# Embedding gates by Strassen's algorithm on 2x2x2 blocks: weight block differences on GpSimd, row block sums on VectorE

## The reference, cut to what matters

```python
h = h + jax.nn.sigmoid(h @ ple_w_gate[i]) * (p[i] @ ple_w_proj[i])
```

## Time and profile before

| what | us |
| --- | --- |
| median of 3 runs | 2815.74 (2813.85 to 2818.06) |
| the profiled execution | 2807.85 |
| its span | 2806.0 |
| TensorE matmuls busy | 2567.0 (91%) |
| VectorE busy | 875.4 (31%) |
| ScalarE busy | 568.4 (20%) |
| GpSimd busy | 480.3 (17%) |
| stage_ple, first and second time, about | 351 to 436 and 858 to 943 |

### The profile page before, as it was taken

The page is one execution under the profiler, slowest core; times in us unless marked ns, Lnnn a source line. Parts: engine busy times, 40 slices in busy tenths (PEclk is TensorE's granted clock), DMA queues, the critical chain, the costliest instruction groups (busy, mean ns, idle before and its releaser), DMA issues. The chain is left out here.

```text
span 2806.0 us, 37484 instructions
## 1 busy us (share of the span) xinstructions
PE 2567.0 (91%) x15258; PEld 1356.2 (48%) x15258; DVE 875.4 (31%) x1809; ACT 568.4 (20%) x1341; POOL 480.3 (17%) x682
## 2 busy tenths in 40 slices
PE   7997898988989999889999999959999899989985
PEld 4654444435554454555555555434455454444442
DVE  2306512353251221664111211120556542111112
ACT  2106112232221111631000010021345111000000
POOL 2623210071231121340000000020344200000001
PEclk9998999997999999999999999979999899999997
DMA  5211013110021420125999999951001089999997
GB/s 177 85 66 46 30 35 120 42 41 2 4 77 37 144 90 32 38 77 209 358 411 411 411 411 411 369 193 53 32 32 61 1 337 411 411 411 411 411 411 282
DMA packets 180273, 532.33 MB, mean 190 GB/s; under 512 B 21360, under 2 KB 31472, under 8 KB 180144
## 3 DMA queue, kind: packets, MB, share of 16 engines
q1 hardware_dynamic: 167536, 505.22, 46.5%
q10 hardware_dynamic: 10240, 16.79, 1.6%
q0 software_dynamic: 2368, 8.52, 0.9%
HBM read 507.26 MB, written 23.10 MB: 189 GB/s over the span
## 5 line engine op out<-in xcount | busy, mean ns | idle before, releaser
L344 PE MATMUL psum<-weight_ring,hidden_T 128*128 128x512 f32 (+2 forms) x1216 | 475.9, 548 | 2.7 <-PEq L576 1.6
L344 PEld LDWEIGHTS psum<-weight_ring,hidden_T 128*128 128x128 f32 x1216 | 228.7, 191 | 223.0 <-issue 158.2
L2982 PE MATMUL psum<-arena,hidden_T 128*64 128x512 f32 x1344 | 296.2, 592 | 0.0
L2971 PEld LDWEIGHTS psum<-hidden_T,arena 128*128 128x128 f32 x2304 | 266.8, 192 | 49.6 <-issue 49.6
L2971 PE MATMUL psum<-hidden_T,arena 128*128 128x128 f32 x2304 | 283.3, 278 | 0.0
L2994 PE MATMUL psum<-weight_ring,hidden_T 128*64 128x512 f32 x1024 | 235.4, 602 | 34.1 <-DMA weight_ring<-in_moe_w_down 30.0
L3248 POOL DMA_INDIRECT arena<-expert_rows_out,arena x18 | 20.4, 1133 | 1061.9 <-issue 534.3
L2982 PEld LDWEIGHTS psum<-arena,hidden_T 128*64 128x64 f32 x1344 | 100.5, 137 | 186.9 <-issue 186.9
L2982 PE MATMUL psum<-weight_ring,hidden_T 128*64 128x512 f32 x704 | 155.0, 592 | 0.0
L2994 PEld LDWEIGHTS psum<-weight_ring,hidden_T 128*64 128x64 f32 x1024 | 71.0, 137 | 153.0 <-issue 128.5
L2976 DVE TENSOR_TENSOR hidden_T<-psum,norm_gains 128x512 f32<-128x512 f32 x64 | 44.3, 691 | 293.9 <-PE psum L2982 182.7
(11 more groups left out here) (546 smaller groups left out, 3195.5 us busy)
## 6 DMA issues: line engine op xcount, KB each, us to landing
arena<-in_moe_w_up SPq DMA_DIRECT2D x84, 2048.0 KB, 24.1
weight_ring<-in_moe_w_down SPq DMA_DIRECT2D x64, 2048.0 KB, 24.0
weight_ring<-in_moe_w_up SPq DMA_DIRECT2D x44, 2048.0 KB, 23.4
weight_ring<-in_hg_w_in SPq DMA_DIRECT2D x8, 2048.0 KB, 10.6
weight_ring<-in_ev_w_in SPq DMA_DIRECT2D x8, 1536.0 KB, 6.9
weight_ring<-in_fox_w_in SPq DMA_DIRECT2D x6, 2048.0 KB, 8.1
weight_ring<-in_od_w_in SPq DMA_DIRECT2D x5, 2048.0 KB, 8.0
weight_ring<-in_ple_w_gate SPq DMA_DIRECT2D x4, 2048.0 KB, 9.3
```

The lines of the kernel that those rows point to most:

```text
L344: last = nc.tensor.matmul(out, l, r, start=i == 0, stop=i == len(left) - 1)
L2971: last = nc.tensor.matmul(g.psum[:, c // 4, (c % 4) * P:(c % 4 + 1) * P], keep[:, i, c * P:(c + 1) * P], row[:, i, :], start=i == 0, stop= ...
L2982: last = nc.tensor.matmul(g.psum[64 * q:64 * q + 64, 2 + n, :].rearrange("p (s c) -> p s c", s=2), xT[:, k // 4, k % 4, ROWS * n:ROWS * n ...
```

## The change

Two column halves of one chunk each, two k halves, and the two tiles of a pair make 2x2x2 blocks; seven products of four k blocks each take the place of eight. The weight differences T[0] to T[3] (128x2048) are made by GpSimd from the ring, behind the root of tile 0 and ahead of its additions to g.h; the row sums S (128x512, four for each pair) by VectorE, two of them between the copies of tiles 2 and 3 to g.hT, the other six behind those of tile 4. Product 1 is copied out of PSUM by ScalarE (first) before product 2 adds to the same bank; the other blocks take it from that copy: VectorE adds it to products 6 and 5 as they come (7 and 4 add in PSUM to bank 2 behind 6, product 3 to bank 3 behind 5), and adds what then stands there for 7, 3 and 4 (take). The sigmoid of six of the eight blocks reads and writes SBUF. Turning uses two banks, 6 and 7, one for each half tile, and its semaphores count halves. The order of TensorE is the list steps. Projections keep their number and size; where each stands changes.

```diff
+    copied, taken, summed, weighted = g.sig("values_copied", "bank_read_by_vector", "block_sums_ready", "weight_sums_ready")
     pT = g.take(2, SEQ)
-    gate, gate2 = g.take(2, 512), g.take(2, 512)
+    T = [g.take(4, 512) for _ in range(4)]
+    S = [[g.take(4, P) for _ in range(4)] for _ in range(2)]
+    first, gates = g.take(2, 512), g.take(8, 512)
...
+    pairs = [(1, 2), (3, 4)]
+    operands = [block_products(row_blocks(g.hT, pair), weight_blocks(g, chunks), S[p], T) for p, pair in enumerate(pairs)]
+    bank = lambda n: g.psum[:, n, :]
+    where = lambda n, p: bank(p) if n < 3 else bank(2) if n in (4, 6, 7) else bank(3)
+    steps = [("turn", "raw", 1), ("turn", "raw", 2), (1, 0), ("turn", "raw", 3), (2, 0), ("turn", "raw", 4), ("proj", 0), (1, 1), (2, 1)]
+    steps += [("turn", "norm", t) for t in few] + [("proj", 1), (6, 0), (5, 0), (7, 0), ("proj", 2), (3, 0), ("proj", 3), (4, 0), ("proj", 4)]
+    steps += [(6, 1), (5, 1), ("turn", "norm", 1), (7, 1), ("proj", 5), ("turn", "norm", 2), (3, 1), ("proj", 6), (4, 1), ("proj", 7), ("turn", "norm", 3), ("turn", "norm", 4)]
...
+    blocks = [(0, 2, 0, 0), (1, 2, 0, 0), (0, 7, 1, 1), (0, 3, 0, 1), (0, 4, 1, 0), (1, 7, 1, 1), (1, 3, 0, 1), (1, 4, 1, 0)]
+    block_at = {block[:2]: e for e, block in enumerate(blocks)}
+    value = lambda p, n: gates[:, block_at[p, n], :]
+    takes = [(n, p) for p in range(2) for n in (6, 5, 7, 3, 4)]
+    taken_at = {job: i + 1 for i, job in enumerate(takes)}
+    sums = [(0, 0), (0, 1), (0, 2), (0, 3), (1, 0), (1, 1), (1, 2), (1, 3)]
...
+                for half in range(2):
+                    j = 2 * turn_at[kind, t] + half
+                    if j >= 2:
+                        pe.wait_ge(*moved.at(j - 1))
+                    for c in range(4 * half, 4 * half + 4):
+                        src = rows[0:n, nth[t] % 2, c * P:(c + 1) * P] if kind == "norm" else g.h[0:n, t, c * P:(c + 1) * P]
+                        last = nc.tensor.transpose(g.psum[:, 6 + half, (c % 4) * P:(c % 4) * P + n], src, g.c("identity")[0:n, 0:n])
+                    last.then_inc(*transposed.up())
+
+            def product(n, p):
+                if n == 1:
+                    pe.wait_ge(*moved.at(2 * turn_at["raw", pairs[p][0]] + 1))
+                if n == 2:
+                    pe.wait_ge(*moved.at(2 * turn_at["raw", pairs[p][0]] + 2))
+                    pe.wait_ge(*copied.at(p + 1))
+                if n == 6:
+                    pe.wait_ge(*weighted.at(2))
+                    pe.wait_ge(*summed.at(4 * p + 2))
+                    if p:
+                        pe.wait_ge(*taken.at(taken_at[4, 0]))
+                if n == 5:
+                    pe.wait_ge(*summed.at(4 * p + 1))
+                    if p:
+                        pe.wait_ge(*taken.at(taken_at[3, 0]))
+                if n == 7:
+                    pe.wait_ge(*weighted.at(3))
+                    pe.wait_ge(*summed.at(4 * p + 3))
+                    pe.wait_ge(*taken.at(taken_at[6, p]))
+                if n == 3:
+                    pe.wait_ge(*summed.at(4 * p + 4))
+                    pe.wait_ge(*taken.at(taken_at[5, p]))
+                if n == 4:
+                    pe.wait_ge(*weighted.at(4))
+                    pe.wait_ge(*taken.at(taken_at[7, p]))
+                a, b = operands[p][n]
+                for k in range(4):
+                    last = nc.tensor.matmul(where(n, p), a[:, k, :], b[:, k, :], start=k == 0 and n in (1, 5, 6), stop=k == 3, skip_group_check=n in (2, 3, 4, 7))
+                last.then_inc(*ready.up())
...
+            def copy(p):
+                act.wait_ge(*ready.at(at[1, p]))
+                nc.scalar.activation(first[:, p, :], bank(p), ACT.Copy).then_inc(*copied.up())
+
+            def sigmoid(e):
+                p, n, i, half = blocks[e]
+                if n == 2:
+                    act.wait_ge(*ready.at(at[2, p]))
+                    nc.scalar.activation(gates[:, e, :], bank(p), ACT.Sigmoid).then_inc(*gated.up())
+                else:
+                    act.wait_ge(*taken.at(taken_at[n, p]))
+                    nc.scalar.activation(gates[:, e, :], gates[:, e, :], ACT.Sigmoid).then_inc(*gated.up())
...
+            copy(0)
+            sigmoid(0)
+            for t in few:
                 scale(t)
-            for t in XT:
-                sigmoid(2 * t - 2)
-                if t > 1:
-                    square(t - 1)
-                sigmoid(2 * t - 1)
-                if t > 1:
-                    scale(t - 1)
+            copy(1)
...
+            def row_sum(p, i):
+                (a11, a12), (a21, a22) = row_blocks(g.hT, pairs[p])
+                s = S[p]
+                if i == 0:
+                    dve.wait_ge(*moved.at(2 * turn_at["raw", pairs[p][1]] + 2))
+                else:
+                    dve.wait_ge(*summed.last())
+                x, y, op = ((a21, a22, ALU.add), (s[0], a11, ALU.subtract), (a11, a21, ALU.subtract), (a12, s[1], ALU.subtract))[i]
+                nc.vector.tensor_tensor(s[i], x, y, op).then_inc(*summed.up())
+
+            def take(n, p):
+                dve.wait_ge(*ready.at(at[n, p]))
+                dve.wait_ge(*copied.at(p + 1))
+                dst = value(p, {6: 3, 5: 7}.get(n, n))
+                if n in (7, 3):
+                    dve.wait_ge(*taken.at(taken_at[{7: 5, 3: 6}[n], p]))
+                nc.vector.tensor_tensor(dst, dst if n in (7, 3) else first[:, p, :], where(n, p), ALU.add).then_inc(*taken.up())
...
+            move("raw", 1)
+            move("raw", 2)
+            row_sum(0, 0)
+            row_sum(0, 1)
+            move("raw", 3)
+            move("raw", 4)
+            for job in sums[2:]:
+                row_sum(*job)
+            multiply(0)
+            for t in few:
+                move("norm", t)
+            multiply(1)
+            for p in range(2):
+                for n in (6, 5, 7, 3, 4):
+                    take(n, p)
+                    if n in (7, 3, 4):
+                        multiply(block_at[p, n])
+                    if p and n == 5:
+                        move("norm", 1)
+                    if p and n == 7:
+                        move("norm", 2)
+            move("norm", 3)
+            move("norm", 4)
 
...
+            def weight_sum(dst, x, y):
+                nc.gpsimd.tensor_tensor(dst, x, y, ALU.subtract).then_inc(*weighted.up())
+
+            (b11, b12), (b21, b22) = weight_blocks(g, chunks)
             for t in few:
                 root(t)
-            for t in XT:
-                add(2 * t - 2)
-                if t > 1:
-                    root(t - 1)
-                add(2 * t - 1)
+            g.weights_wait(pool, chunks[0])
+            g.weights_wait(pool, chunks[1])
+            weight_sum(T[0], b12, b11)
+            pool.wait_ge(*weighted.at(1))
+            weight_sum(T[1], b22, T[0])
+            weight_sum(T[2], b22, b12)
+            pool.wait_ge(*weighted.at(2))
+            weight_sum(T[3], b21, T[1])
+            for e in range(5):
+                add(e)
...
```

More of the change, by code:

```diff
@@ L583, in turn @@
                     pe.wait_ge(*scaled.at(nth[t] + 1))
[L584 to L591, removed]
@@ new lines, in project @@
+            def project(e):
+                p, _, i, half = blocks[e]
+                a = TILES[pairs[p][i]][0] - META
+                if e >= 2:
+                    pe.wait_ge(*multiplied.at(e - 1))
+                w = g.weights(proj_chunk)
+                products(nc, bank(4 + e % 2), [pT[:, k, a:a + P] for k in range(2)], [w[:, k, 512 * half:512 * half + 512] for k in range(2)]).then_inc(*proj_ready.up())
+            for s in steps:
+                if s[0] == "turn":
+                    turn(*s[1:])
+                elif s[0] == "proj":
+                    if s[1] == 0:
@@ L604, in _ @@
                         g.weights_wait(pe, proj_chunk)
                         pe.wait_ge(*p_in.at(16))
[L606 to L616, removed]
+                    project(s[1])
+                else:
+                    if s == (1, 0):
+                        g.weights_wait(pe, chunks[0])
+                    product(*s)
+                    if s == (4, 0):
+                        g.chunk_used(chunks[0], ready)
+                    if s == (3, 1):
+                        g.chunk_used(chunks[1], ready)
@@ L647, in _ @@
                 square(t)
+            copy(0)
+            sigmoid(0)
+            for t in few:
                 scale(t)
-            for t in XT:
-                sigmoid(2 * t - 2)
-                if t > 1:
-                    square(t - 1)
-                sigmoid(2 * t - 1)
-                if t > 1:
-                    scale(t - 1)
+            copy(1)
+            for e in (1, 2, 3, 4):
+                sigmoid(e)
+            square(1)
+            square(2)
+            scale(1)
+            scale(2)
+            sigmoid(5)
+            sigmoid(6)
+            square(3)
+            sigmoid(7)
+            scale(3)
             square(4)
```

(6 more changed lines are left out.)

73 lines of the change are left out of this document (23 added, 50 removed).

## The result

| | before | changed |
| --- | --- | --- |
| median, us | 2816.45 (2813.85 to 2818.06, 4 runs) | 2799.81 (2798.76 to 2800.86, 4 runs) |
| ratio | | 0.9942, 95% interval 0.9925 to 0.9959 |
| the profiled execution, us | 2807.85 | 2800.86 |
| its span | 2806.0 | 2799.1 |
| first gate stage, first turning to the next stage's first product | 351.64 to 435.81: 84.17 | 352.68 to 430.83: 78.15 |

The changed kernel is faster, by 16.6 us in these medians, where 9.6 had been forecast. The two profiled executions differ by 7.0 us only, the two gate stages by 6.02 + 4.01 = 10.03.

A forecast was written before the change was run, and what follows sets the result against it. The gate stage was taken as a TensorE chain; 5.80 and 3.83 us saved in two stages, together 9.6, took the profiled 2807.85 to 2798.2, plus 7.9 carried over gave 2806.1 us; range 2802.0 to 2811.0.

The forecast's parts named there:

- Removed work: Gate products on TensorE: 8 fewer matmuls of 0.429 us per pair of tiles, 6.86 us less per stage, 13.7 for two.
- The weight difference: One GpSimd subtraction of 128x2048 in the gate stages: 4.28 us, bounds 3.66 and 5.06.
- The walk: TensorE's queue stepped through each gate stage to the last product's end: 67.43 us in the first, 70.19 in the second.
- Exclusion: GpSimd and VectorE, both inputs in SBUF, take turns by whole instructions; 1.07 us excludes at 512 elements; PSUM copies aren't held.
- no-exclusion rival: Row sums beside differences aren't held up; only 0.86 us lost per stage, gain 13.0, time 2802.7 us; chance 0.20.
- long-differences rival: GpSimd's weight differences take 5.06 us each; gain 4.7 us, time 2811.0; chance 0.08.
- the slower one: Exclusion by elements stretches each difference beside VectorE to 8.3 us; time 2831 us; chance 0.05.
- The two waits before tile 4: TensorE idle before turning tile 4, whose turning needs tile 3's copies behind row sums: 0.65 us first stage, 2.75 second.
- The wait for product 1's copy: TensorE waits before product 2 of pair two for ScalarE's copy of product 1: 0.86 us.
- The tail: From a gate stage's last product to the next stage's first product: the same chain, 10.94 us unchanged.
- part (3): Among what is added in the gate stages: turning a tile handed over by halves, through two banks in place of four.
- The rival's price: Clock rival: second stage's pause before tile 4 costs TensorE its clock, 1.8 us; gain 7.8, time 2807.9; chance 0.25.

The follow-up runs named there:

- the pieces: Each of GpSimd's four 128x2048 weight differences made as four 128x512 instructions, against the changed kernel; 2795.33 us, ratio 0.9939 to the kernel before.
- the kernel that copies first: VectorE copies tiles 3 and 4 before any row sum, against the changed kernel; 2797.71 us, ratio 0.9949 to the kernel before.
- the third: Third profiled execution of the changed kernel, from its third timing with no edit: 2799.99 us, ratio 0.9959 to the kernel before; second stage 82.57 us.

## Why the prediction was wrong

In the stages the mechanism was right. The result fell 2.2 us below the range, mostly by the last step of the sum, which goes from the gain to the median, and for the rest because the gain came out larger.

**Which step failed.** "The median of the runs shown is 2815.74, 7.9 above that execution; the difference is carried over: 2806.1 us." It did not carry over. The changed kernel's median, 2799.81, lies 1.05 us below its profiled execution (2800.86) and not 7.9 above it. This step is 8.9 us too high; the profiled execution itself came out 2.7 us above its forecast of 2798.2, and 6.3 us remain between 2806.1 and 2799.8.

Both ends of the 7.9 were off. The profiled execution of the kernel before was a short one outside the two stages, 2637.0 us against 2642.9 in its second. And the level of 2815.74 came from three runs: 55 later runs of the same kernel, in three groups, have medians of 2810.4 to 2812.5. With 2812.3 the same sum gives 2802.7, inside the range. Counted so, 3.4 of the 6.3 us are level and 2.9 are gain: the stages of the changed kernel save 10.03 where I had 9.6, and the measured gain stands above the stages' by what the section before leaves open. Counted against the kernel before timed beside it (2816.45), all of the miss is gain, 16.6 for 9.6; the later groups, which give 13.8 together, speak for the first count. Why the first group's level is some 4 us above the others isn't shown.

**Removed work**: right. 112 matmul records in place of 128 in each stage, those on sums at 0.43 us as well (24 in 10.46).

**The weight difference**: 4.28 us taken; it is recorded at 4.52 (bounds 3.66 and 5.06), and at 4.84 to 4.96 where a row sum is still running as it starts. The walk came out right nevertheless, because what it used was the part that holds VectorE: row sum 2 took 4.89, 4.21 more than its own 0.68, and 4.28 is four times the 1.07 of the earlier trace rows. The record is 0.3 us longer than the hold; at 512 elements it is 0.2 (1.27 and 1.07). The Trainium skill (GPSIMD Engine Reference, section 3.1) states 4497 ns for an addition of this size; the traces agree, 4.50 to 4.53 us for the subtraction wherever no row sum is running as it starts.

**Exclusion**: right, and shown by the pieces and by the kernel that copies first; what the one row sum of 4.06 us waited for stays open. The no-exclusion rival falls, since row sums took 4.88. The long-differences rival falls too, since the hold was 4.21 and not 5.06, and so does the slower one, for which a difference had to take 7.2.

**The two waits before tile 4**: 0.53 and 2.46 us for 0.65 and 2.75. **The wait for product 1's copy**: 0.95 for 0.86. Nothing else waited. Walk to the last product: 67.78 for 67.43, and 924.61 - 854.10 = 70.51 for 70.19.

**The tail**: "so 10.94 us stay" failed by 0.57. In the changed kernel the last product ends at 420.46 and the next stage begins at 430.83: 10.37. The chain is the same up to the last turning (7.33 us before, 7.35 after). From there it is 435.81 - 432.20 = 3.61 before and 3.02 after. The last turning of the kernel before:

```profile
432.20 1.97 PE L588 MATMUL psum<-constants,arena 128*128 128x128 f32 x8 [4.35 <-ACT arena L644]
```

In the changed kernel VectorE copies the first half as soon as its four transposes are done:

```profile
428.96 0.69 DVE L725 TENSOR_TENSOR hidden_T<-psum,norm_gains 128x512 f32<-128x512 f32 x1 [3.87 <-PE psum L601]
429.82 0.69 DVE L725 TENSOR_TENSOR hidden_T<-psum,norm_gains 128x512 f32<-128x512 f32 x1 [0.16 <-PE psum L601]
```

I had listed the handing over by halves as part (3) and given it no gain. It is 1.1 us for the two stages, and makes up for 0.7 that the walk was too short.

**The clock** "at 1.00 up to the tail in both stages": so in the first two executions, not in the third. The rival's price was right, 1.70 us for 1.8; its pause was 2.07 us and not 2.6.

**The range** was too narrow for what it rested on. It added bounds of the costs in the stages to a level known from three runs, and allowed 0.7 us for the spread on its low side.

## What to carry to other kernels

Forecast the difference and the level apart: here the difference was off by 4 of 14 us, the level by 3.4, and the level had been given no width. One execution can lie 6 us off outside the stages that changed, so the lengths of those stages are the better measure of a small change. Before work goes to a second engine to spare the first, look whether the first has time at that place; here 9.2 us of differences fitted in idle VectorE time, and the second engine's long two-input instructions held up copies that the matmul engine was waiting for. Where two engines exclude each other, put the copies that feed the matmul engine ahead of the sums that are needed later, and cut the long instruction.

## What the runs showed of the hardware

- GpSimd's 128x2048 subtraction, fp32: 4.50 to 4.53 us where no row sum of VectorE is running as it starts, 4.84 to 4.97 where one is; VectorE 2.28 to 2.29. A 128x512 one in a row of four: 1.25 to 1.27 alone.
- A VectorE sum of two SBUF inputs waits for about 4.2 us of such a GpSimd instruction; two copies from PSUM to SBUF beside it take 1.28, as alone.
- Of four GpSimd instructions back to back, VectorE's sum once got in only behind the last (4.06 us), and in fifteen cases behind one or none (0.90 to 1.75).
- The same idle 2.07 to 2.08 us of TensorE was followed by the lower clock in two profiled executions and not in three others of the changed kernel and its variants.
- TensorE can stop for 1.9 to 3.2 us among independent matmuls while weight loads fill the DMA engines (share 0.98 to 1.07, 362 to 397 GB/s; 0.62 in the last microsecond of the longest); the place moved from after 19 to after 46 of 80 equal matmuls when the instruction stream was made 201 instructions longer.
